# Cache copies in 4 KB pieces and on another queue, transposes a step later, tokens in four loads: one decoder layer on one core

## What is computed

```
proj  = h @ w_in                                   # q, k, v, z, xBC, dt
att   = dilated attention over windows (128,1),(512,4),(2048,16), merged
        # samples: over a cache of 2048 keys and values per sequence
ssm   = gated_rmsnorm(ssd_scan(silu(conv(xBC)), dt, ...), z)   # chunks of 128
h1    = layer_norm(ALPHA*h + concat(att, ssm) @ w_out)
q     = h1 @ w_q ; s = q @ sub_keys                # 8 heads, 2 halves of 128 keys
e     = the 16 best of 128*128 experts per head
y     = layer_norm(ALPHA*h1 + sum gate * gelu(h1 . u[e]) * v[e])
also returned: both caches (8 x 2048 x 1024 values each), moved on by 4 positions
```

## Time and profile before

| | |
|---|---|
| median of 3 runs | 2130.69 us (2120.62 to 2135.42) |
| the profiled execution | 2130.82 us, its span 2129.0 us |
| PE busy | 2029.7 us (95%) |
| mean granted clock of TensorE | 0.978 of full speed |
| moved by the DMA engines | 683.04 MB, mean 321 GB/s |

### The profile page before, as it was taken

The page is one execution under the profiler, slowest core; times in us unless marked ns, Lnnn a source line. Parts: engine busy times, 40 slices in busy tenths (PEclk is TensorE's granted clock), DMA queues, the critical chain, the costliest instruction groups (busy, mean ns, idle before and its releaser), DMA issues.

```text
span 2129.0 us, 33458 instructions
## 1 busy us (share of the span) xinstructions
PE 2029.7 (95%) x12130; PEld 1687.5 (79%) x12130; DVE 1481.9 (70%) x3108; ACT 744.1 (35%) x1112; POOL 781.4 (37%) x483
## 2 busy tenths in 40 slices
PE   7998999998889999899999999999989999999998
PEld 7998975555453348899999999999977877777776
DVE  1375125554573335579889699999788889888988
ACT  2232113444341002124343355555433333333332
POOL 4342310000110003247889732222365555555630
PEclk9999999999989999999999999999999999999999
DMA  9998877787998579837999878887999999999993
GB/s 328 341 307 319 311 279 300 315 354 253 339 329 331 162 262 352 312 124 269 346 362 356 312 279 306 300 306 279 382 401 389 392 392 392 392 386 387 386 363 138
DMA packets 202351, 683.04 MB, mean 321 GB/s; under 512 B 18305, under 2 KB 84225, under 8 KB 194177
## 3 DMA queue, kind: packets, MB, share of 16 engines
q1 hardware_dynamic: 150256, 442.42, 57.6%
q0 software_dynamic: 46080, 167.79, 20.6%
q10 hardware_dynamic: 5904, 71.39, 9.7%
HBM read 618.78 MB, written 196.32 MB: 383 GB/s over the span
## 4 chain that ended last, share of the span: by engine, by line
PE 56%; DMA 21%; issue 9%; DVE 8%; POOL 3%; ACT 2%; SPq 0%; POOLq 0%; DVEq 0%; ACTq 0%
DMA overlay<-peer_v 16%; PE bank L188 11%; PE bank L189 10%; PE bank L190 10%; PE bank L1474 5%; PE bank L2076 4%; POOL overlay L363 3%; DVE overlay L2288 2%; PE bank L666 2%; DVE arena L2089 2%; PE bank L682 2%; DMA overlay<-peer_wq 2%; DMA overlay<-peer_u 1%; PE bank L732 1%; ACT overlay L2196 1%
## 5 line engine op out<-in xcount | busy, mean ns | idle before, releaser
L188 PE MATMUL bank<-overlay 128*128 128x384 f32 (+4 forms) x2768 | 943.7, 341 | 37.5 <-DVE overlay L2294 18.9
L189 PE MATMUL bank<-overlay 128*128 128x384 f32 (+4 forms) x2768 | 928.5, 335 | 0.0
L190 PE MATMUL bank<-overlay 128*128 128x384 f32 (+4 forms) x2768 | 927.8, 335 | 0.0
L188 PEld LDWEIGHTS bank<-overlay 128*128 128x128 f32 (+1 forms) x2768 | 522.6, 189 | 86.6 <-issue 36.4
L190 PEld LDWEIGHTS bank<-overlay 128*128 128x128 f32 (+1 forms) x2768 | 522.0, 189 | 31.4
L189 PEld LDWEIGHTS bank<-overlay 128*128 128x128 f32 (+1 forms) x2768 | 522.7, 189 | 30.1
L1913 POOL DMA_INDIRECT arena<-peer_v,arena x160 | 258.0, 1613 | 226.5 <-DVE arena L2089 213.1
L1634 POOL TENSOR_TENSOR overlay<-overlay 128x1024 fp32r<-128x1024 f32 x86 | 206.7, 2404 | 291.9 <-ACT overlay L1627 288.3
L2089 DVE SCALAR_TENSOR_TENSOR arena<-arena 128x1024 f32<-128x1024 f32 x160 | 205.3, 1283 | 0.1
L1627 ACT CAST overlay<-overlay 128x1024 fp32r<-128x1024 f32 x144 | 150.1, 1044 | 157.5 <-DMA overlay<-peer_u 87.1
L1913 POOL DMA_INDIRECT arena<-peer_rows,arena x80 | 109.9, 1373 | 243.4 <-DVE arena L2084 223.8
(11 more groups left out here) (239 smaller groups left out, 2176.4 us busy)
## 6 DMA issues: line engine op xcount, KB each, us to landing
overlay<-peer_u SPq DMA_DIRECT2D x128, 512.0 KB, 7.9
overlay<-peer_v SPq DMA_DIRECT2D x128, 512.0 KB, 11.7
o_vsall<-cache_vall SPq DMA_DIRECT2D x22, 2044.0 KB, 27.2
o_ks<-cache_k ACTq DMA_DIRECT2D x10, 4088.0 KB, 17.9
arena<-cache_kT SPq DMA_DIRECT2D x32, 896.0 KB, 11.2
arena<-cache_v SPq DMA_DIRECT2D x56, 512.0 KB, 6.6
arena<-w_out SPq DMA_DIRECT2D x48, 512.0 KB, 5.6
act<-arena SPq DMA_DIRECT2D x128, 192.0 KB, 8.4
```

Source lines behind the costliest of these rows:

```text
L188: pe.matmul(out, lhs[0], rhs[0], start=start, stop=False)
L189: pe.matmul(out, lhs[0], rhs[1], start=False, stop=False)
L190: return pe.matmul(out, lhs[1], rhs[0], start=False, stop=stop)
```

## The change

Six edits stand in the diff.

1. All cache copies are cut into runs of 1022 float32 values, 4088 bytes (`PIECE = CHUNK // 128`), whichever queue they go by. A key piece is now 128 x 8 runs, a value half 64 x 8.
2. In the projection ACT issues a quarter of a key piece and a quarter of a value half behind each block, not one of each behind every fourth.
3. Four value halves move from SP's queue at the end of the attention to ACT's in rounds 47, 51, 55 and 59; the 13 of the queries move from SP's queue to ACT's, one behind each of the first 13 queries.
4. In the state-space loop PE's `turn_out` of a chunk comes behind the next chunk's `state` (for the last one behind the samples' first `intra`), and DVE waits for `ssm_norm_g` only where it first uses it.
5. `dec_turn_out` comes last in its round.
6. The tokens are loaded in four pieces of two slices, behind `w_dt`, which is now the first load and the first thing that ACT and DVE split.

```diff
-        PIECE = CHUNK // 16
+        PIECE = CHUNK // 128
-        def copy_cache(eng, side, x):
+        def copy_part(eng, side, at, n):
             src, dst = (("cache_k", "o_ks"), ("cache_vall", "o_vsall"))[side]
-            cutout = lambda ap, lo: ap.rearrange("b s d -> b (s d)")[:, bass.ds(x * CHUNK + lo, CHUNK)]\
-                .rearrange("b (s n) -> s b n", n=PIECE)
+            cutout = lambda ap, lo: ap.rearrange("b s d -> b (s d)")[:, bass.ds(at + lo, n)].rearrange("b (s n) -> s b n", n=PIECE)
             eng.dma_start(cutout(t[dst], 0), cutout(t[src], NT * D)).then_inc(copied, 16)
+        def copy_cache(eng, x):
+            copy_part(eng, 0, x * CHUNK, CHUNK)
         def copy_half(eng, y):
+            copy_part(eng, 1, y * (CHUNK // 2), CHUNK // 2)
...
         def sp_project(sp):
-            sp.dma_start(xraw[:, 0:4], t["xT"][:, 0:4]).then_inc(x_in[0], 16)
             sp.dma_start(dtw_raw, t["w_dt"]).then_inc(dtw_in, 16)
-            sp.dma_start(xraw[:, 4:8], t["xT"][:, 4:8]).then_inc(x_in[1], 16)
+            for k in range(4):
+                sp.dma_start(xraw[:, 2 * k:2 * k + 2], t["xT"][:, 2 * k:2 * k + 2]).then_inc(x_in[k], 16)
...
-            def copies(x):
-                copy_cache(act, 0, x)
-                copy_half(act, x)
+            def copies(x, s):
+                copy_part(act, 0, x * CHUNK + s * (CHUNK // 4), CHUNK // 4)
+                copy_part(act, 1, x * (CHUNK // 2) + s * (CHUNK // 8), CHUNK // 8)
             for s in range(4):
                 hi(0, s, (feat_ready, s + 1))
-            copies(0)
+                copies(0, s)
...
             for c in range(DC):
-                pe.wait_ge(x_lo, 5 if c < 4 else c + 2)
+                pe.wait_ge(x_lo, c + 2)
...
-            for y in range(15, 19):
-                copy_half(sp, y)
...
             for n in range(ROUNDS):
+                if n in (47, 51, 55, 59):
+                    copy_half(act, 15 + (n - 47) // 4)
...
+            def turn_normed(i):
+                dve_ssd.wait(pe, i, "t_inter")
+                pe_ssd.count_done(i, "out_turned", turn_out(pe, i - 1, 0))
             for i in range(QT):
                 state(i)
+                if i >= 2:
+                    turn_normed(i - 1)
                 intra(i, 0)
...
                 seg(i + 1, 1)
-                if i:
-                    dve_ssd.wait(pe, i, "t_inter")
-                    pe_ssd.count_done(i, "out_turned", turn_out(pe, i - 1, 0))
             intra(QT, 0)
+            turn_normed(QT - 1)
...
         def dve_ssd_run(dve):
-            dve.wait_ge(normg_in, 16)
...
                 dve_ssd.wait(dve, i, "rstd")
+                if i == 0:
+                    dve.wait_ge(normg_in, 16)
...
         def sp_query(sp):
-            copy_half(sp, 19)
             with sp.Fori(1, QF // 4) as k:
                 for s in range(4):
-                    copy_half(sp, k * 4 + (16 + s))
                     sp.wait_ge(u_lo, k * 4 + (s - 3))
...
+            with act.Fori(0, QF // 4 - 1) as k:
                 for s in range(4):
+                    query(k, s)
+                    copy_half(act, k * 4 + (19 + s))
```

More of the change, by code:

```diff
@@ L244, in layer @@
         consts_in, dtw_in = sem("consts_in"), sem("dtw_in")
-        x_in = [sem(f"x_in{s}") for s in range(2)]
+        x_in = [sem(f"x_in{s}") for s in range(4)]
         x_hi, x_lo = sem("x_hi"), sem("x_lo")
@@ L339, in act_project @@
                     hi(x, s, (feat_ready, x * 4 + (s + 1)))
-                copies(x)
+                    copies(x, s)
             act_dt(act)
@@ L346, in act_project @@
                         silu(act, x * 3 + s)
-                copies(x + 4)
+                    copies(x + 4, s)
             with act.Fori(0, 2) as x:
@@ L350, in act_project @@
                     hi(x + 8, s, (rows_ready, x * 10 + (5 if s < 2 else 10)))
-                copies(x + 8)
+                    copies(x + 8, s)
             for s in range(4):
@@ L366, in pool_project @@
                 lo(0, s)
-            pool.wait_ge(x_in[0], 16)
-            pool.wait_ge(x_in[1], 16)
+            for k in range(4):
+                pool.wait_ge(x_in[k], 16)
             pool.tensor_copy(xsam, xraw[:, :, SEQ:]).then_inc(sam_in, 1)
@@ L755, in pe_attend @@
                         dec_scores(b, 2 * at + 1)
-                    if at == EVERY + 4:
-                        dec_turn_out(b)
                 if 2 <= n < UNITS + 2:
@@ L768, in pe_attend @@
                     values(n - 3)
+                for b, at in sample_steps(n):
+                    if at == EVERY + 4:
+                        dec_turn_out(b)
         def dve_attend(dve):
@@ L1695, in act_query, with query @@
             act.sem_inc(q_kept, 2)
-            with act.Fori(0, QF // 4) as k:
-                for s in range(4):
-                    f = k * 4 + s
-                    act.wait_ge(q_ready, f + 1)
-                    act.wait_ge(s_ready, f + 1)
-                    act.copy(qT[:, s % 2].rearrange("p (h n) -> p h n", h=2), bank[:, 2 * (s % 2):2 * (s % 2) + 2, 0:HALF]).then_inc(q_kept, 1)
-                    hi_of(act, s, k + 1)
+            def query(k, s):
+                f = k * 4 + s
+                act.wait_ge(q_ready, f + 1)
+                act.wait_ge(s_ready, f + 1)
+                act.copy(qT[:, s % 2].rearrange("p (h n) -> p h n", h=2), bank[:, 2 * (s % 2):2 * (s % 2) + 2, 0:HALF]).then_inc(q_kept, 1)
+                hi_of(act, s, k + 1)
+            with act.Fori(0, QF // 4 - 1) as k:
+                for s in range(4):
+                    query(k, s)
+                    copy_half(act, k * 4 + (19 + s))
+            for s in range(4):
+                query(QF // 4 - 1, s)
+                if s == 0:
+                    copy_half(act, 31)
             for g in range(1, FOLD):
```

26 lines of the change are left out of this document (11 added, 15 removed).

## The result

| | before | changed |
|---|---|---|
| median | 2133.06 us (4 runs, 2120.62 to 2141.67) | 3034.94 us (4 runs, 3010.13 to 3058.82) |
| profiled execution, span | 2129.0 us | 3008.3 us |
| granted clock | 0.978 | 0.840 |
| moved, mean rate | 683.04 MB, 321 GB/s | 683.05 MB, 227 GB/s |

The ratio is 1.421 (95% interval 1.413 to 1.429). The forecast was 2090 us, its range 2074 to 2115: wrong in sign and far outside. Nearly all of the miss is one price, that of a 4088-byte run; what is left when it is taken out stands in the second part of the experiments. One of the four executions of the changed kernel was in a slower state, as were the profiled one of e3_before_short and three of the four of e1_shift4 further down (which has no ratio for that reason); ratios and intervals go by the others.

The account below looks back on a forecast made before the run. It took PE's chain of waits as the bound, the DMA-busy last stage as fixed. Terms 2.0 + 11.3 + 4.0 + 12.0 + 3.8 - 2.0 + 9.1 = 40.2 us off 2130.82 gave 2090 us, range 2074 to 2115.

Parts of the forecast that it names:

- turn-taking arithmetic: Loads beside copies: engines alternate between queues run by run, so 8 x (copy run + load run) plus latency; about 6 us.
- price of a short run: All cache copies: a 4088-byte run holds a DMA engine 0.190 us, at the long runs' 21.5 bytes per ns.
- signs of being wrong: ACT-queue packets above 0.2 us, ACT issues above 1 us delaying casts, PE waiting for `w_out`, costly half-clock spells at new places.
- rival C: Projection and middle: short runs are dear and ACT sticks issuing, so slower; 2187 us at 0.28 us per run; chance 0.07.
- 24T + 1.3: Projection: DMA time in us a block asks per engine, T per short copy run; 5.9 at 0.19, 7.1 at 0.24.
- Start, 2.0: Start: loading tokens in four pieces lets `w_dt` products begin after one slice; 2.0 us gained, at most 2.3.
- Projection, 11.3: Projection: earlier `w_in` loads remove PE's 8.1 us wait and about 3.2 us of half clock; bounds 0 and 13.2.
- Attention, 4.0: Attention: `dec_turn_out` placed last in its round saves 4.0 of PE's 5.1 us wait; bounds 0 and 5.1.
- State space, 12.0 + 3.8, and -2 behind it: `ssm_norm_g` wait removed gains 12.0 us, two `turn_out` waits 3.8; later `w_out` loads take back 2 (bounds 0 and 12).
- Queries, 9.1: Queries: copies on another queue in small runs let loads land in about 6 us; 9.1 us gained, bounds 0 and 10.
- rival A: Projection and queries: the queue makes no difference, loads stay as late; 20 us gained, 2111 us; chance 0.12.
- Rival B: Middle: SP's copies, if short runs are a tenth slower, make PE wait for `w_out`; 2100 to 2103 us; chance 0.17.

Follow-up runs that it names:

- e3_before_short: The kernel before with every copy cut into 4088-byte runs, same queues and places of issue: 3008.51 us, ratio 1.409.
- e1_shift4: The changed kernel with 4096-byte copy runs, every run starting 16 bytes later than aligned, on both sides: 3555.06 us (3485 to 3621).
- e2_long: The changed kernel with the earlier 32,704- and 16,352-byte runs, projection copies again behind every fourth block: 2132.41 us, ratio 1.0011.
- e13: The kernel before with only the state-space edits, `ssm_norm_g` awaited at first use and `turn_out` a step later (also spelled e13_statespace): 2130.62 us, ratio 1.0001.
- e4_before_odd: The kernel before with its long runs shortened by 8 bytes, so most start off alignment: 2321.81 us, ratio 1.0885.
- e7_dst_odd: The changed kernel with 4096-byte copy runs, read side aligned, written side 8 bytes later: 3425.29 us, ratio 1.5841.
- e1_aligned: The changed kernel with aligned 4096-byte copy runs in place of 4088-byte ones, same queues and places of issue: 2238.55 us, ratio 1.0485.

## Experiments: where the rest of the forecast went

With the runs long, the change gains nothing (e2_long, ratio 1.0011), where the terms without the projection's still promise 28.9 us. The stage table shows both sides: state space 12.5 us less and queries 8.7 less, but attention 22.1 and the output product 5.8 more.

**e5_sp_halves: e2_long with the four halves of the attention given back to SP.**

```diff
+            for y in range(15, 19):
+                copy_half(sp, y)
...
-                if n in (47, 51, 55, 59):
-                    copy_half(act, 15 + (n - 47) // 4)
```

Expected: 

> The change with long runs (2132.41 us), with the four value halves of attention given back to SP's queue behind the attention's loads; the load of the state-space norm stays late. If these halves on ACT's queue are what made attention 22 us longer there (their runs beside the loads of values, PE waiting 12.7 us for them): attention comes back to about 218 us and the whole to 2110 us (2106 to 2116). If the 22 us came from something else that moved (dec_turn_out a round later, the clock): it stays at 2128 to 2136 us.

**e6_16k: the same with key runs of 16,352 bytes, spread over the blocks.**

```diff
-            copy_part(eng, 0, x * CHUNK, CHUNK, PIECE)
+            copy_part(eng, 0, x * CHUNK, CHUNK, PIECE // 2)
...
-                if s == 3:
-                    copy_cache(act, x)
+                if s in (0, 2):
+                    copy_part(act, 0, x * CHUNK + s * (CHUNK // 4), CHUNK // 2, PIECE // 2)
+                if s == 1:
                     copy_half(act, x)
```

Expected: 

> The kernel before this one in the list, with key copies in runs of 16,352 bytes instead of 32,704, spread in the projection over the blocks (half a key piece behind the first and third block of four, a value half behind the second). These are the shortest runs of the kernel before, which are as fast per byte as its longest. By turn-taking of the queues, a load of w_in (8 runs of 4 KB per engine) then waits 8 x (0.73 + 0.17) = 7.2 us and some latency instead of 13.5: it lands in about 11 us, the PE wait of 8.1 us at the first rows product goes, and so does some of the slow clock. About 2100 us (2094 to 2108). If the wait there has another cause, or the clock takes the time back: 2108 to 2114 us, as without it.

Measured (before: 2119.94 us on that chip): e5 2113.27 us, ratio 0.9977 (0.9959 to 0.9995); e6 2126.45, ratio 1.0024 (1.0000 to 1.0048). The waits of PE in e2_long, then in e5_sp_halves:

```profile
PE bank L727 <- DMA arena<-cache_v: 12.7, 6, 5.2
```

```profile
PE bank L1477 <- DMA arena<-w_out: 14.0, 2, 9.3
...
PE bank L431 <- POOL overlay L361: 4.2, 4, 1.7
...
PE bank L729 <- DMA arena<-cache_v: 1.4, 2, 1.1
```

Attention is back at 217.2 us and PE's wait for `cache_v` down from 12.7 to 1.4, so the halves on ACT's queue did hold up the loads of the values. I had priced them by ACT's time of issue, and not by the loads beside them. In the whole they are worth about 7 us (1.0011 to 0.9977, and the two intervals overlap by a little), not 22: some of the stage time came from that one execution (e13, with the attention of the kernel before, had 226.1), and SP's queue is fuller in front of `w_out` now (14.0 us of waits). e6 missed: `w_in` landed at 15.6 us at the median, not 11, and the whole is 10 us slower than e5. Why isn't settled; the turn-taking arithmetic, which had fitted one landing time, does not predict another well.

**e12_queries and e13_statespace: one part of the change each, on the kernel before.**

```diff
         def sp_query(sp):
-            copy_half(sp, 19)
...
-                    copy_half(sp, k * 4 + (16 + s))
...
         def act_query(act):
...
+                    copy_half(act, k * 4 + (19 + s))
...
```

```diff
         def pe_ssd_run(pe):
...
             for i in range(QT):
                 state(i)
+                if i >= 2:
+                    turn_normed(i - 1)
...
         def dve_ssd_run(dve):
-            dve.wait_ge(normg_in, 16)
...
```

Expected of the queries: 

> The kernel before with the query stage's part of the change alone: the value halves on ACT's queue behind each query, in the runs of the kernel before. The prediction's term for that stage: 9.1 us less, ratio 0.9957. The rival that a queue makes no difference: ratio 1.000. Its stage (first query score to last) falls from 115.6 to 107 us by the first.

Expected of the state space: 

> The kernel before with the state-space part alone: DVE waits for ssm_norm_g only where it uses it, and turn_out comes a step later; copies as before. The prediction's terms: 12.0 and 3.8 less, 2.0 to 12 back at w_out: 4 to 14 us less, ratio 0.9935 to 0.998, if the loads ahead give back more than forecast; 0.9935 by the prediction. If ACT and PE are held by something else there: 1.000.

Measured (before: 2130.10 us there): queries alone 2123.73 us, ratio 0.9973 (0.9947 to 0.9998), their stage 124.8 us for 133.8 (131.2 in e13, where it is not edited); state space alone 2130.62 us, ratio **1.0001** (0.9974 to 1.0028). The second is the most telling. PE in e13_statespace, its waits (first in total, then in time with the products behind them), and the stretches 600 to 640 us (length, busy and count, clock, DMA, GB/s):

```profile
PE bank L1479 <- DMA arena<-w_out: 16.6, 2, 12.1
```

```profile
640.97 10.07 PE L1479 MATMUL bank<-arena 128*128 128x512 f32 x16 [12.14 <-DMA arena<-w_out]
656.39 5.40 PE L1479 MATMUL bank<-arena 128*128 128x512 f32 x8 [4.49 <-DMA arena<-w_out]
```

```profile
600.00:620.00 20.00, 16.24 (x77) 0.91 1.01 319
620.00:640.00 20.00, 8.27 (x52) 0.50 0.98 345
```

The waits of 12.0 and 7.7 us are gone (0.7 each is left), PE comes earlier, and stands 16.6 us before `w_out`, 12.1 of them for its first block; the kernel before shows no such wait. The first output product starts 109.8 us after the front for 115.2, and both stages together take 278.9 us for 277.7. If the copies ahead of `w_out` are the bound of that place, taking them away must take the wait away. Three more kernels move them.

**e8_slack, e9_between, e11_five: copies taken from in front of `w_out`.** Each is e5_sp_halves with the value halves 11 to 14 elsewhere: e8 (halves 10 to 14 and one key piece) among the last loads, e9 behind every third of the middle ones, e11 as e9 but one load sooner, and with the sixth key piece there too, in two parts.

```diff
-                if i < 2:
-                    copy_half(sp, 2 * i + 11)
-                    copy_half(sp, 2 * i + 12)
...
             for c in range(16):
                 weights(c + 8)
+                if c in (2, 5, 8, 11):
+                    copy_half(sp, 11 + (c - 2) // 3)
```

(This is e9.)

Expected of e8_slack: 

> The change with long runs and SP's four attention halves (2113.27 us, ratio 0.9977), with the value halves 10 to 14 and the last key piece taken from before and between the first w_out loads and put among the later ones, from 700 us on, where the DMA engines are half idle (0.47 to 0.62). If the copies ahead of w_out are what took back the gain of the state-space stage: PE's 14.0 us of waits for w_out go, with some of the slow clock of that stretch (0.59 and 0.73 over 40 us, 14 us lost at most): 12 to 22 us less, 2092 to 2102 us, ratio 0.988 to 0.993. If another wait stands behind it (the samples' key and value copies of SP are no more than that, or the moved copies now delay w_out later or the queries): 2108 to 2116 us.

Expected of e9_between: 

> The change with long runs and SP's four attention halves (2113.27 us, ratio 0.9977), with the value halves 11 to 14 taken from between the first w_out loads and put singly behind every third of the next loads (650 to 720 us, where a load is issued eight tiles ahead of its use), not in one burst with a key piece at 730 to 750 us as in the kernel before this (2130.31 us, 20.5 us of waits there). If what fails there is only the burst: PE's waits for w_out fall under 3 us, 2096 to 2106 us against a kernel before at 2120 (ratio 0.988 to 0.994). If six key pieces ahead of w_out are enough to make it late, or the clock takes the time back: 2108 to 2116 us (ratio 0.996 to 1.000).

Expected of e11_five: 

> The kernel with the four value halves between the later w_out loads (2110.12 us, ratio 0.9922), and now also the sixth key piece there, in two parts. If the six key pieces ahead of w_out make the wait of 12.0 us: 4.19 MB less at some 330 bytes per ns are 12 us, the wait goes, 2094 to 2102 us against a kernel before at 2120 to 2130 (ratio 0.984 to 0.989). If the freed time is taken elsewhere (later loads, clock): ratio 0.991 to 0.995.

| | us | before there | ratio (95%) | state space + output | waits for `w_out` |
|---|---|---|---|---|---|
| e8_slack | 2130.31 | 2126.75 | 1.0020 (0.9984 to 1.0057) | 287.8 | 20.5 |
| e9_between | **2110.12** | 2128.92 | **0.9922** (0.9895 to 0.9949) | 271.6 | 12.0 |
| e11_five | **2108.73** | 2130.10 | **0.9898** (0.9855 to 0.9942) | 265.8 | 3.7 |

The stretches of e8_slack, then those of e9_between:

```profile
680.00:700.00 20.00, 20.00 (x43) 1.00 0.45 158
...
740.00:760.00 20.00, 11.43 (x39) 0.86 1.01 362
```

```profile
680.00:700.00 20.00, 20.00 (x42) 1.00 0.78 283
...
740.00:760.00 20.00, 20.00 (x76) 1.00 0.63 217
```

e8 put the copies behind loads that go out in bursts of four; they came too late and in a heap, and left the idle stretch idle. e9 fills it, and e11 takes most of the last wait away. Both beat the kernel before and the changed one. The intervals of e9 and e11 overlap. e11 is 21.7 us (12.4 to 30.9) faster than before; the forecast's terms for what it keeps of the change, all but the projection's, are 28.9. Between the profiled executions state space and output took 11.9 us less (forecast 13.8) and the queries 8.8 (9.1), while the attention shows nothing of its 4.0 (222.0 us). So most of the forecast was there to be had, once the copies were moved too.

## Why the prediction was wrong, point by point

**The step that failed is the price of a short run**: "I hold to 0.190, since long runs and gathers differ by only an eighth per byte". Measured 0.467. Both witnesses were blind to what counts: the long runs start and end at multiples of 32, and the gathers read rows of DRAM and do not write it. I had seen that "each run also starts at an odd address" and gave it 3%, by a rule on reading. Of the signs of being wrong that it named, these came: packets above 0.2 us, issues of ACT above 1 us with casts behind them, and a wait for `w_out`; the granted clock fell as well, from 0.978 to 0.840. The bound "from above, unknown" should have kept far more than 0.07 for rival C.

**Rival C was the truth in kind.** ACT stuck in issues, casts behind them, SP 202 us for six key pieces. Its size was not: its own formula, 24T + 1.3, gives 12.5 us per block at T = 0.467, 40 x 6.4 = 256 us for the projection, of which it let some 25 fit into the queue, where 355 came. It kept the loads at 0.167, while they took 0.39: 24 x 0.467 + 8 x 0.39 = 14.3 us per block, 40 x 8.2 = 328 us more, which is most of it. And it priced the projection and the middle alone; attention grew by 120.2 us and the queries by 149.5. For aligned runs the formula fits, if nothing is taken off for the queue: 24 x 0.251 + 1.3 = 7.3 for 6.1, 40 x 1.2 = 48 us, and 46.6 were measured.

**Start, 2.0**: right. The first feature product starts at 16.6 to 16.9 us in all the profiled kernels that have the edit and long runs, and at 19.15 to 19.7 in those that have not, and the 48th stays as far ahead (22.8 us in e2_long, 25.05 before). In the length of the whole projection (long runs) it drowns: 300.9 to 305.9 us with it, 301.6 to 307.7 without.

**Projection, 11.3**: not to be had. `w_in` landed in 24.2 us, not 6. With aligned runs it was 11.0, but the copies then asked for more than the time of a block. Short runs can cut a load's delay; what they take of the engines is the price. Turn-taking at the measured packets gives 8 x (0.467 + 0.39) = 6.9 us, so the step from a packet's time to a landing time failed too; up to four loads stand in the queue at once, which it left out. And the 8.1 us were no fixed sum: with the same projection PE waited there 3.7 us in e12_queries and 6.0 in e13_statespace.

**Attention, 4.0**: `dec_turn_out` waits no more, but no gain shows. With the halves back on SP's queue (e5) the stage took 217.2 us for 217.9, and the waits at the transposes of the prompt's scores grew from 4.9 to 6.7 us. The edit of the four halves, entered as 0 because ACT had time, cost about 7 us. The term looked at the engine that issues and not at the loads in whose way the copies come.

**State space, 12.0 + 3.8, and -2 behind it**: the waits went as forecast (of `turn_out` 7.7 less the 0.7 left and the 3.4 that went to `intra`: 3.6 for 3.8). The give-back was mis-sized: not 2 but all of the 15.8, within the 6 us that the interval of e13 (1.0001) leaves either way. "PE comes 16 us earlier, the loads 11: 5 us of the slack are used up" reckoned with the fifth block, from the longest landing time of any load in that stretch; in e13 PE waits for the first block (12.1 us) and the third (4.5). The bound of -12 that I had entered was nearly the value.

**Queries, 9.1**: right in size, by half of its mechanism. The stage is 8.7 to 9.0 us shorter than in the kernel before in every kernel that has the edit with long runs; in the whole it is 5.8 us (0.4 to 11.3) as a single edit. But the loads landed in 12.3 us at the median of all 16 in e12_queries, for 25.2 before, and not in 6: the runs there are the long ones, and it was enough that no copy stood ahead of a load on its own queue. That also speaks against rival A, that the queue makes no difference.

**Rival B**, that SP's copies bound the middle, was right at the old price already, as e13, e9 and e11 show together, and not only if runs got dearer. It had 0.17.

## What to carry to other kernels

Before a copy is cut anew, take its run's length and its start modulo 32 bytes on the side that is *written*: an edge that cuts a 32-byte unit cost some 0.2 us of a DMA engine here, about as much again as a whole 4 KB run, while on the side that is read it cost nothing. Where no row shows a price, and the address differs in kind from all that do, keep the chance for the dear case, and price it in every stage where the copies run, with what the loads beside them lose. When a wait is taken away in front of a load that stands behind bulk copies, the bulk copies are the bound: move them into a stretch with idle DMA engines, one by one between loads issued well ahead, in the same edit.

## What the runs showed of the hardware

- A DRAM-to-DRAM run with one partly written 32-byte unit at an edge takes 0.42 to 0.46 us for 4 KB, with two 0.63 to 0.73, with none 0.22 to 0.25 (20 to 140 us). With the 4088-byte runs, 1.5 such edges on average, it was 0.47 in the changed kernel and 0.66 in e3_before_short. Loads of 4 KB that share the engines go from 0.16 to 0.39 us meanwhile in the changed kernel.
- The fee does not grow with the run's length: 0.33 us for 1.5 edges on runs of 16 and 32 KB (e4_before_odd).
- DMA engines busy for nine tenths of the time or more moved 90 GB/s with two such edges (20 to 140 us of e7_dst_odd), 267 with none (e1_aligned), and 327 with long runs (e2_long). A busy share alone says nothing about the rate.
- Behind such copies an engine stands in the issue itself: 0.6 us of ACT became up to 37.8, and 1.6 us per key piece of SP's became 34.
